# Output projection of a three-branch attention layer: the two column halves taken in turn, product by product

## The reference

```
y = concatenate([rms_normalize(oa), rms_normalize(ob), rms_normalize(oc)], axis=-1)
y = y * g_branch * silu(z)
y = einsum('bse,ed->bsd', y, w_out)          # 1024 x 1024 by 1024 x 1024
x = layer_norm(ALPHA * x + y, ln_gain, ln_bias)
```

## Time and profile before

| | |
|---|---|
| median of 3 timed runs | 569.33 us (569.31 to 569.79) |
| span of the profiled execution | 567.9 us |
| PE busy | 539.9 us, 95% of the span |
| DVE, ACT, POOL busy | 59%, 48%, 25% |
| chain that ended last | PE 85%, DVE 7%, ACT 3% |
| matmuls, weight loads | 3808, 3808 |
| output projection (L728) | 384 products of 512 columns, from 344.7 to 559.4 us |

### The profile page before, as it was taken

How to read it: one execution, slowest core, us unless ns; L and a number is a source line. 1 busy time by engine, 2 the same in 40 slices (tenths; PEclk the granted TensorE clock), 3 DMA queues, 4 the chain that set the end, 5 groups by cost and what they waited for, 6 DMA issues and landing times.

```text
span 567.9 us, 10755 instructions
## 1 busy us (share of the span) xinstructions
PE 539.9 (95%) x3808; PEld 495.5 (87%) x3808; DVE 335.7 (59%) x1000; ACT 273.1 (48%) x729; POOL 143.6 (25%) x148
## 2 busy tenths in 40 slices
PE   4999899999999999999999998999999999989994
PEld 3989899999999988888888787898789988979983
DVE  3687851286775124545545577776867666575543
ACT  4242330311010035566576599676667666756631
POOL 0030333641130010222202222152415240241325
PEclk9999999999999999999999999999999999999997
DMA  8934020512020001111011164002010202020021
GB/s 270 317 113 122 1 75 1 168 56 75 1 75 1 1 1 39 38 38 39 7 33 38 42 223 181 2 1 76 14 63 1 75 1 76 1 75 2 2 75 74
DMA packets 28788, 35.37 MB, mean 62 GB/s; under 512 B 3520, under 2 KB 22464, under 8 KB 28736
## 3 DMA queue, kind: packets, MB, share of 16 engines
q1 hardware_dynamic: 28736, 34.69, 18.6%
HBM read 30.49 MB, written 4.19 MB: 61 GB/s over the span
## 4 chain that ended last, share of the span: by engine, by line
PE 85%; DVE 7%; ACT 3%; issue 2%; DMA 1%; SPq 0%; POOLq 0%; POOL 0%; DVEq 0%; ACTq 0%
PE long_ps L728 13%; PE o_ps L695 10%; PE wide L570 10%; PE wide L572 10%; PE wide L571 10%; PE narrow L680 6%; PE long_ps L630 4%; PE long_ps L632 4%; PE long_ps L631 4%; PE wide L669 3%; PE wide L668 3%; PE narrow L644 2%; DVE nb L1054 2%; ACT prob L843 1%; PE long_ps L547 1%
## 5 line engine op out<-in xcount | busy, mean ns | idle before, releaser
L570 PE MATMUL wide<-w_hi,x_hi 128*128 128x256 f32 x448 | 129.1, 288 | 0.0
L571 PE MATMUL wide<-w_lo,x_hi 128*128 128x256 f32 x448 | 127.4, 284 | 0.0
L572 PE MATMUL wide<-w_hi,x_lo 128*128 128x256 f32 x448 | 127.4, 284 | 0.0
L571 PEld LDWEIGHTS wide<-w_lo,x_hi 128*128 128x128 f32 x448 | 86.8, 194 | 0.0
L570 PEld LDWEIGHTS wide<-w_hi,x_hi 128*128 128x128 f32 x448 | 86.7, 194 | 0.0
L572 PEld LDWEIGHTS wide<-w_hi,x_lo 128*128 128x128 f32 x448 | 86.6, 193 | 0.0
L843 ACT ACTIVATE prob<-prob,nb 128x256 f32<-128x256 f32 (+7 forms) x96 | 55.8, 582 | 56.4 <-DVE nb L1054 36.4
L1016 DVE SCALAR_TENSOR_TENSOR q_lo<-narrow,q_hi 128x256 fp32r<-128x256 f32 x80 | 29.6, 371 | 78.7 <-ACT q_hi L827 78.7
L1142 POOL TENSOR_TENSOR w_lo<-w_raw,w_hi 128x1024 fp32r<-128x1024 f32 x16 | 38.6, 2440 | 105.2 <-ACT w_hi L768 105.2
L827 ACT ACTIVATE q_hi<-narrow 128x256 fp32r<-128x256 f32 x80 | 26.4, 330 | 66.0 <-PE narrow L644 66.0
L857 ACT ACTIVATE prob_t<-narrow 128x512 f32<-128x512 f32 (+3 forms) x96 | 49.1, 528 | 16.4 <-PE narrow L680 15.9
(11 more groups left out here) (115 smaller groups left out, 1176.2 us busy)
## 6 DMA issues: line engine op xcount, KB each, us to landing
w_raw<-in_w_in SPq DMA_DIRECT2D x14, 512.0 KB, 5.1
rows<-in_x SPq DMA_DIRECT2D x16, 256.0 KB, 7.1
g_raw<-in_w_in SPq DMA_DIRECT2D x8, 512.0 KB, 3.7
wo_raw<-in_w_out SPq DMA_DIRECT2D x8, 512.0 KB, 3.9
res<-in_x SPq DMA_DIRECT2D x8, 512.0 KB, 3.3
out<-res SPq DMA_DIRECT2D x7, 512.0 KB, 2.6
w_raw<-in_w_mem SPq DMA_DIRECT2D x4, 512.0 KB, 4.2
rows<-in_mem SPq DMA_DIRECT2D x4, 256.0 KB, 3.0
```

What stands on the lines that cost most here:

```text
L570: pe.matmul(dst, t_hi[:, k, cols], w_hi[s][:, k, :], start=(k == 0), stop=False)
L571: pe.matmul(dst, t_hi[:, k, cols], w_lo[s][:, k, :], start=False, stop=False)
L572: mm = pe.matmul(dst, t_lo[:, k, cols], w_hi[s][:, k, :], start=False, stop=(k == KT - 1))
```

## The change

In every block the list of products now runs over branches, tiles and splittings, and innermost over the two halves. Two neighbours share the stationary operand (`y_hi` or `y_lo` of one tile) and write to the two banks in turn. The splittings come in the order 0, 2, 1. Half 0 of a block therefore ends one product before half 1, so that its residual on DVE is due in the last iteration of the block, for every block.

```
-RES_AT = [{i: OUT_AT[i] + (n if i in BY_BRANCH else -(-n // 2)) - 1 for i, n in enumerate(OUT_ITERATIONS)},
+RES_AT = [{i: OUT_AT[i] + n - 1 for i, n in enumerate(OUT_ITERATIONS)},
           {i: OUT_AT[i] + n for i, n in enumerate(OUT_ITERATIONS)}]
...
 def out_order(i):
 
-    halves_of = [[0, 1]] if i in BY_BRANCH else [[0], [1]]
-    return [(half, k, p) for halves in halves_of for tiles in BRANCH_TILES
-            for half in halves for k in tiles for p in range(3)]
+    return [(half, k, p) for tiles in BRANCH_TILES for k in tiles for p in (0, 2, 1) for half in range(2)]
```

## The result

| | before | after |
|---|---|---|
| median | 569.50 us (4 runs) | 587.71 us (586.15 to 588.78, 4 runs) |
| ratio | | 1.0312, 95% interval 1.0293 to 1.0332 |
| span of the profiled execution | 567.9 us | 587.0 us |
| mean granted clock in it | 0.995 | 0.987 |

Slower by 3.1%, 18.2 us. The direction and the place were as forecast, the size was not: 14.4 had been forecast, and the median lies 0.2 above the end of the stated range. The profiled execution itself took 588.78 us, 1.8 more than its span.

The account below looks back on a forecast made before the run. PE was taken as the bound; 0 + 12.7 + 0.8 + 0.5 - 0.8 + 1.2 = +14.4 us on the 567.9 span gives 582.3, or 583.7 us as timed median. The range was 578 to 587.5.

Parts of the forecast that it names:

- step 1: The 384 output-projection products: shared stationary operand and alternating banks change nothing, 0 us, bounds -3.3 and +1.9.
- step 2: Start of all eight blocks: PE's second product waits until DVE empties half 1's bank, +12.7 plus 0.8 us.
- step 3: Blocks 1 to 6: half 0's residual moves to the last iteration, making DVE late, +0.5 us (-0.5 to +1.5).
- step 4: Output-projection stretch: PE's 5.3 us of waits for exponentials shrink behind the new waits, -0.8 us.
- step 5: End of the kernel: DVE reaches half 1's residual later, after half 0's residual and statistics, +1.2 us.
- rival C: After each new stop at a block's start, five products run at 1.2 GHz: +9.2, 593 us; chance 4%.
- A (shared loads pay): Output projection: waits as forecast, but each pair's second product loses its overhead, -3.3, giving 580.4 us; chance 7%.
- B (the waits don't bind): Block starts: half 1's residual is in time for the second product, while pairs save 3.3: 566 us; chance 2%.
- D (much more is given back): Output-projection stretch: all 5.3 us of waits for exponentials is eaten, sum 9.9, giving 579.2 us; chance 4%.

Follow-up runs that it names:

- block 0 alone: The kernel before, with only block 0 taking the two halves in turn: 573.25 us, ratio 1.0074.
- the run with the filled wait of block 0: The kernel with only block 0 taking the halves in turn, plus six extra products ahead of that block's first: 571.12 us, ratio 1.0033.
- the last but one experiment: The kernel before, with blocks 1 to 6 taking halves in turn throughout and DVE's residual of half 1 first in its iteration: 569.74 us, ratio 1.0011.
- block 3 alone: The kernel before, with only block 3 taking the two halves in turn: 571.33 us, ratio 1.0033.
- block 7 alone: The kernel before, with only block 7 taking the two halves in turn: 571.45 us, ratio 1.0037.
- the lead version: The kernel before, blocks 1 to 6 having nine products of half 0, 30 in turn, nine of half 1: 568.46 us, ratio 0.9986.

## Why the prediction was right, and where its sizes were off

**Products, step 1.** Right: 0. The mean distance between neighbours of L728 or L726, leaving out those above 0.245, is 0.2305 to 0.2307 us in the kernel before, and 0.2305 to 0.2306 in the changed one, whether the stationary operand stays or changes. The trace has a load for each product in both kernels; what it would bring to leave one out, no run here shows. The Trainium skill (TensorE: Matmul & The Clock Gate, "Step-by-step: what each phase is for") says that one can load once and multiply repeatedly. The trace does not show that done.

**Start of a block, step 2.** The mechanism was right in all eight places: PE stands at the second product until DVE has emptied the bank. The step reckoned 12.7 plus 0.8. The second product of blocks 0 to 7 now starts 2.32, 2.22, 2.26, 2.09, 1.70, 2.26, 2.12 and 1.71 us behind the first; less 0.23 each, that is 14.8. Of the 1.3 missing, 0.4 is the handing over: PE starts about 0.15 after DVE's end (406.87 to 407.01 at block 2), where 0.1 was estimated. The other 0.9 is in blocks 1 and 7, where the residual of half 1 ends 0.5 and 0.4 later behind PE's first product than before. In blocks 2 to 6 it ends where it did, to 0.01. The step had said that nothing on DVE ahead of this residual depends on the moved products. That is wrong in these two places, where the residual of half 0 stands ahead of it and waits for products that have moved.

**Residual of half 0, step 3.** The step looked in the wrong places, and that the 0.9 above is near its +0.5 is luck. The move counted in six blocks costs nothing, alone (1.0005) or in the timeline of blocks 2 to 5, and gives back 0.3 in block 4, which lies inside the step's lower bound. It sticks out at block 7: there the residual of half 0 of block 6 waits for PE's last products (it starts at 564.01, its statistics at 564.74), and no scores stand between in which DVE would wait for PE anyway. And it sticks out at block 1, which the step did not count: there the residual kept its iteration, but block 0's half 0 had been complete six products before the end and is now complete one before. By itself this moves DVE by 0.2 only. The rest comes from a small addition of DVE, which stands ahead of the residual and now starts just behind the start of an instruction of POOL instead of just ahead of it. The changed kernel, and the kernel before:

```profile
375.36 0.74 POOL L1168 TENSOR_TENSOR y_lo<-zt,y_hi 128x256 fp32r<-128x256 f32 x1 [2.25 <-ACT y_hi L900]
375.48 0.63 DVE L1065 TENSOR_TENSOR den_all<-den,gap_exp 128x2 f32<-128x2 f32 x1
```

```profile
370.50 0.15 DVE L1067 TENSOR_TENSOR den_all<-den,gap_exp 128x2 f32<-128x2 f32 x1
370.51 0.74 POOL L1170 TENSOR_TENSOR y_lo<-zt,y_hi 128x256 fp32r<-128x256 f32 x1 [2.24 <-ACT y_hi L902]
```

DVE's instruction takes 0.63 us instead of 0.15 and ends 0.01 behind that of POOL.

**Given back, step 4.** Waits for exponentials fell from 5.3 to 4.7, 0.6 against 0.8 forecast. Right.

**The end, step 5.** 1.6 us from last product to residual instead of 0.5: +1.1, against 1.2. Right.

**The clock, rival C.** This is the term that the sum lacked. I had called it a rival with a chance of 4%, on the ground that PE had stopped for 1.3 us before with a full clock, and the range had no room for it. The runs show it as part of the answer. Filling the waits with products takes 4.3 us off the changed kernel and 2.1 off the one with block 0 alone. Its size can be read block by block in the profiled execution of the changed kernel, from the starts of the blocks in the timeline of PE. Blocks 0, 1 and 3 (block 2, at 404.75, stands above):

```profile
345.06 0.40 PE L726 MATMUL long_ps<-wo_hi,y_hi 128*128 128x512 f32 x1
...
375.76 0.39 PE L726 MATMUL long_ps<-wo_hi,y_hi 128*128 128x512 f32 x1
...
436.85 0.40 PE L726 MATMUL long_ps<-wo_hi,y_hi 128*128 128x512 f32 x1
```

Each block's length goes from its first product to that of the next, block 7's to its last product; "second product later" is the wait, by starts; "rest" is what the block grew beyond it (us):

| block | before | after | longer | second product later | rest |
|---|---|---|---|---|---|
| 0 | 26.26 | 30.70 | 4.44 | 2.09 | 2.35 |
| 1 | 26.78 | 28.99 | 2.21 | 1.99 | 0.22 |
| 2 | 29.06 | 32.10 | 3.04 | 2.03 | 1.01 |
| 3 | 28.38 | 30.33 | 1.95 | 1.86 | 0.09 |
| 4 | 34.16 | 35.31 | 1.15 | 1.47 | -0.32 |
| 5 | 38.40 | 39.67 | 1.27 | 2.02 | -0.75 |
| 6 | 20.64 | 22.69 | 2.05 | 1.89 | 0.16 |
| 7 | 11.05 | 12.50 | 1.45 | 1.39 | 0.06 |

The two blocks with a dent of the clock have a rest of 2.35 and 1.01, together 3.4 us; the six others together have -0.5, about the 0.6 that is given back. With 1.1 at the end and 0.4 by which block 0 starts later, ahead of anything that was changed, this is the whole 19.1 between the two spans. Without the clock and these 0.4 it would be 15.3, against 14.4 forecast.

I had looked at the longest single wait of PE, and not at what stood just ahead of block 0 in the timeline of PE, before:

```profile
341.42 1.08 PE L695 MATMUL o_ps<-v_c,prob_t 128*128 128x64 f32 x8 [0.36 <-DVE qo L1075]
...
343.70 0.66 PE L680 MATMUL narrow<-ident,prob 128*128 128x128 f32 x4 [1.21 <-ACT prob L843]
```

Two stops, 0.36 and 1.21 us idle, lie within 4 us ahead of the new one of 1.92, and they can bring the clock down without it, as the run with the filled wait of block 0 shows. The Trainium skill (TensorE: Matmul & The Clock Gate, "A second HAM failure mode: psum-queue depth-cycling") tells of cycling through banks together with small idle times between the groups, and doesn't part the two. Here the cycling alone does no harm: with 288 products in turn and no waits (the last but one experiment) the clock stayed full in the profiled execution.

The runs of single blocks add up to nearly the same: block 0 alone +4.2, block 3 alone +1.9, block 7 alone +2.1, and five more blocks at block 3's price 9.5, together 17.7 of 18.2. The share of the five was not run by itself; in the table they grew by 9.7.

**Rivals A, B and D.** A (shared loads pay) and B (the waits don't bind) did not happen; D (much more is given back) neither.

## What to carry to other kernels

Two accumulators filled in turn are both needed at the first step and both released at the last: the time in which one was emptied behind the other's products is lost, at each change of block and at the end. Before such a reordering, take for each buffer the end of the release and the start of its first use from the timelines; the difference, summed over all places, was here most of the answer. And look at the stops that stand close to the new ones: at block 0, right behind two stops of 0.36 and 1.21 us, the new one came with a fall of the clock that cost as much again (2.35 beside 2.09). Whether it would have done so without them was not run.

## What the runs showed of the hardware that I had not expected

In the profiled execution of the changed kernel the granted clock fell to half 1.0 us before the end of the stop at block 0 (at 346.4; PE's next product starts at 347.38), for 6.8 us, and for 3.4 us behind the one at block 2 (idle 1.92 and 1.87); it stayed full behind stops of nearly the same length at blocks 1, 3, 5 and 6 (1.82, 1.69, 1.87 and 1.74). Why block 2 and not those is open. In the run with the filled wait of block 0 it fell for 3.4 us behind stops of 0.35 and 1.21 us alone. The kernel before seems to have its share of it, though its one trace shows no dent: of the 23 executions run beside block 0 alone, four have a mean clock of 0.994 and take 570.8 to 571.2 us, while those with 0.995 to 0.997 take 568.7 to 569.7. The clock doesn't explain that the lead version read 1.0 below. Counting only executions with a mean clock of 0.996 or more, its median is 568.35 (9 of 12) against 569.23 (17 of 23) for the kernel before, and 568.58 (6 of 12) against 569.23 (17 of 20) when it was run again. Of the 1.2 us between the spans of the profiled executions of the first lead version and of the kernel before, 0.9 lie ahead of block 0, where the program is the same (343.76 against 344.67), and 0.3 in block 4. The start of block 0 moves between 343.45 and 345.42 in the profiled executions of all versions. A small gain is not excluded, and not shown. An effect below 2 us in a single run of this kernel can be nothing.

DVE's small addition (`den_all`), 0.15 us in the median, took 0.63 in block 1 of the changed kernel, where it starts 0.12 us into an instruction of POOL, and ended 0.01 us behind that. In the kernel before the same happens at 401.00, 457.93 and 492.60: it starts 0.10 us into POOL's `y_lo`, takes 0.65 us and ends 0.02 behind it. No run was made on its cause.

Alternating between two PSUM banks from product to product, at 512 columns each, costs nothing that the timeline shows: 0.23 us a product in both orders.
